# The second kind's attention heads beside the first kind's key and value projections, and the routed rows' queries in plain float32 with ten gather buffers

## The reference, cut to what matters

```python
# 1. first block, attention: two kinds of heads, each 8 heads of 128
q_nope, q_pe = split(rms(cq) @ wq_b)              # first kind: queries, 128 + 64 wide
k_nope, v    = split(rms(ckv) @ wkv_b)            # first kind: keys and values, projected from 512
y_a = softmax(q_a @ k_a.T * A_SCALE) @ v          # first kind
y_b = softmax(q_b @ k_b.T * B_SCALE) @ v_b        # second kind: q_b, k_b, v_b are ready before wkv_b
out = (concat(y_a, y_b) * silu(gate)) @ w_out     # then x = layer_norm(ALPHA * x + g * out)

# 2. last layer of the second block: each row picks 128 expert rows out of 16384
q   = hn @ peer_w_q                               # 2048 -> 8 heads x 128
s1, s2 = q @ sub_keys                             # per head: 2 lists of 128, top 16 of each,
idx = top 16 of the 256 sums                      # 16 experts a head, 128 a row
act = gelu(hn . u_tab[idx]); out = sum(g * act * v_tab[idx])   # 2 x 256 gathers of 128 rows of 8 KB
```

## Time and profile before

| | us |
|---|---|
| median of 3 runs (3640.46 to 3644.57) | 3642.04 |
| profiled execution, its own time | 3634.11 |
| its span | 3632.8 |
| mean granted TensorE clock | 0.864 |

### The profile page before, as it was taken

The page is one execution under the profiler, slowest core; times in us unless marked ns, Lnnn a source line. Parts: engine busy times, 40 slices in busy tenths (PEclk is TensorE's granted clock), DMA queues, the critical chain, the costliest instruction groups (busy, mean ns, idle before and its releaser), DMA issues.

```text
span 3632.8 us, 35860 instructions
## 1 busy us (share of the span) xinstructions
PE 2654.2 (73%) x13396; PEld 2054.7 (57%) x13396; DVE 2679.2 (74%) x3835; ACT 1080.2 (30%) x2010; POOL 1525.5 (42%) x1943
## 2 busy tenths in 40 slices
PE   7989999887999999799978998414434443444445
PEld 6868897455999988598767887401111111111112
DVE  8977887667566655578846555699797888888775
ACT  2255252243444444444664544200000000000000
POOL 7887778740000000000000000277777776767663
PEclk9999999998999999899999999757677766776668
DMA  9876767345376645443124544599999999999998
GB/s 369 319 252 234 247 224 259 144 140 179 107 253 247 219 149 185 174 163 117 70 81 140 185 140 144 199 408 422 422 421 421 416 421 412 423 421 416 422 422 338
DMA packets 277678, 974.09 MB, mean 268 GB/s; under 512 B 14464, under 2 KB 30464, under 8 KB 208384
## 3 DMA queue, kind: packets, MB, share of 16 engines
q0 software_dynamic: 76592, 551.58, 36.8%
q1 hardware_dynamic: 198560, 411.70, 32.4%
q10 hardware_dynamic: 2352, 8.52, 0.7%
HBM read 957.06 MB, written 14.68 MB: 267 GB/s over the span
## 4 chain that ended last, share of the span: by engine, by line
PE 40%; POOL 25%; DMA 17%; DVE 11%; issue 5%; ACT 2%; ACTq 0%; DVEq 0%; POOLq 0%
DMA ring<-in_peer_v,arena 11%; POOL ring L3142 8%; PE lin L486 6%; PE lin L488 6%; PE lin L489 6%; PE lin L2906 5%; PE lin L449 4%; PE lin L450 4%; PE lin L451 4%; DMA ring<-in_peer_u,arena 3%; PE lin L2278 3%; DMA phases<-phase 3%; DVE ring L3063 2%; POOL phase L952 2%; POOL phase L947 2%
## 5 line engine op out<-in xcount | busy, mean ns | idle before, releaser
L2906 PE MATMUL lin<-ring,diag 128*128 128x512 f32 x768 | 535.5, 863 | 732.7 <-DMA ring<-in_peer_v,arena 566.1
L410 DVE TENSOR_TENSOR weight_parts<-ring,weight_parts 128x512 fp32r<-128x512 f32 (+2 forms) x1074 | 709.8, 674 | 489.2 <-ACT weight_parts L398 483.7
L398 ACT CAST weight_parts<-ring 128x512 fp32r<-128x512 f32 (+2 forms) x1074 | 635.7, 599 | 831.1 <-PE lin L489 431.0
L2906 PEld LDWEIGHTS lin<-ring,diag 128*128 128x128 f32 x768 | 207.5, 284 | 1056.0 <-issue 880.0
L3063 DVE CUSTOM_DVE_ANT_0 ring<-ring,arena 128x2048 f32<-128x2048 f32 x256 | 583.4, 2289 | 159.2 <-DMA ring<-in_peer_u,arena 150.9
L486 PE MATMUL lin<-parts,weight_parts 128*128 128x256 f32 x2112 | 611.5, 290 | 47.8 <-DVE weight_parts L410 47.8
L3142 POOL DMA_INDIRECT ring<-in_peer_u,arena x256 | 440.9, 1722 | 402.8 <-DVE arena L2997 254.8
L488 PE MATMUL lin<-parts,weight_parts 128*128 128x256 f32 x2112 | 604.0, 286 | 0.0
L489 PE MATMUL lin<-parts,weight_parts 128*128 128x256 f32 x2112 | 603.8, 286 | 0.0
L3142 POOL DMA_INDIRECT ring<-in_peer_v,arena x256 | 470.9, 1840 | 247.0 <-PE lin L2906 174.6
L2638 POOL DMA_DIRECT2D arena<-mem_keys x1 | 0.6, 575 | 1257.4 <-DVE weight_parts L410 1257.4
(11 more groups left out here) (284 smaller groups left out, 3298.3 us busy)
## 6 DMA issues: line engine op xcount, KB each, us to landing
ring<-in_ada_w SPq DMA_DIRECT2D x96, 1024.0 KB, 8.2
ring<-in_w_in_fourier SPq DMA_DIRECT2D x64, 1024.0 KB, 7.8
ring<-in_w_kv_mem SPq DMA_DIRECT2D x32, 1024.0 KB, 7.7
ring<-in_w_in_attn SPq DMA_DIRECT2D x32, 1024.0 KB, 5.5
ring<-in_w_out_fourier SPq DMA_DIRECT2D x16, 2048.0 KB, 8.0
ring<-in_w_in SPq DMA_DIRECT2D x24, 1024.0 KB, 5.1
ring<-in_w_out_attn SPq DMA_DIRECT2D x8, 2048.0 KB, 8.1
ring<-in_w_out SPq DMA_DIRECT2D x8, 2048.0 KB, 8.1
```

Of the source, the lines that this page charges most:

```text
L398: c.nc.scalar.copy(c.w_parts[:, q, 0, 0:w], c.slot(load, L.kc, w)[:, k % L.kc, :]).then_inc(c.a_high.after(("high", L.name, i)), 1)
L410: c.nc.vector.tensor_tensor(c.w_parts[:, q, 1, 0:w], c.slot(load, L.kc, w)[:, k % L.kc, :], c.w_parts[:, q, 0, 0:w].bitcast(F32), ALU.subt ...
L2906: mm = nc.tensor.matmul(X.sums[t][b][:, :], c.diag[:, X.diag_of(t, k), :], X.bufs[gather_buf(n)][:, b * 512:(b + 1) * 512], start=(k == PE ...
```

## The change

First part. The order of the heads is turned: place n runs head `head(n)`, so places 0 to 7 are the second kind and 8 to 15 the first. Places 0 to 7 stand beside the projections: each has 5 steps of side work, the two key matmul groups or the two value groups of a pair of heads, 5 more steps, and then the place's own head. The rope moves behind place 0, the turns of the queries into places 6 and 7. The later places have 3 + 3 steps for 2 + 2. The scores run one head ahead in places 0 to 7 and two ahead later. SP loads a projection's weights and five (before: four) `ada_w` blocks in turn. The parts of y are split behind places 9, 10 and 13, only part 1 inside `w_out_attn`. x is loaded onto the residual's place, and only the first block's output waits for it.

Second part. The rows are turned first, all 16 blocks; the four query groups use `pe_cols`, each load one unit of the ring. The choice of heads 0 and 1 runs with nothing between, on DVE. The gathers take ten buffers from the first on: four that are free and six ring units as the query groups are done with them. The steps of a choice stand at k = 0, 2, … 18.

```diff
+def head(n):
+    return (n + HEADS) % (2 * HEADS)
 def sp_attention(c):
     for g in range(HEADS // 2):
         yield from sp_load(c, ("wkv_b", g), ...)
-        yield from sp.aside(16)
+        yield from sp.aside(4 * SLOT_STEPS)          # SLOT_STEPS, HEAD_STEPS = 5, 3
...
 def pe_attention(c):
     yield from pe_split_rows(c, X.wq_b, ("cq",), X.cq_rows)
+    yield from pe_scores(c, X, 0)
+    for n in range(HEADS):
+        g = n // 2
+        yield from pe.aside(SLOT_STEPS)
+        yield from (pe_values if n % 2 else pe_keys)(c, X, g)
+        yield from pe.aside(SLOT_STEPS)
+        if n == HEADS - 1:
+            yield from pe_turn(c, "q_pe", ...)
+        yield from pe_turn_probs(c, X, n)
+        if n == HEADS - 2:
+            yield from pe_turn(c, "q_nope", ..., [("attn", "q_roped")])
+        if n == HEADS - 1:
+            yield from pe.wait_ge(*turn_free("q_nope", 8, NT), *turn_free("q_pe", 8, NT), ...)
+        yield from pe_scores(c, X, n + 1)
+        yield from pe_mix(c, X, n)
+    yield from pe_scores(c, X, HEADS + 1)
...
 def v_attention(c):
+    yield from v_scores(c, X, 0)
+    yield from v_normalise(c, X, 0)
+    for n in range(HEADS):
+        yield from v.aside(SLOT_STEPS)
+        yield from v_copy_out(c, key, ...)           # of the keys or the values
+        yield from v.aside(SLOT_STEPS)
+        yield from v_turned_probs(c, X, n)
+        yield from v_scores(c, X, n + 1)
+        yield from v_mixed(c, X, n)
+        yield from v_normalise(c, X, n + 1)
+        if n == 0:
+            ...                                      # rope of the queries
+    low = v_residual_parts(c, c.attn_out.R)
+    for n in range(HEADS, 2 * HEADS):
+        yield from v_turned_probs(c, X, n)
+        ...
+        yield from v.aside(HEAD_STEPS)
+        yield from v_mixed(c, X, n)
+        yield from v.aside(HEAD_STEPS)
+        if n in PART_AFTER:                          # {9: 2, 10: 3, 13: 0}
+            yield from low(PART_AFTER[n])
...
 def g_attention_out(c):
-    yield from c.g.wait_ge(("free", ("mix", 2 * HEADS - 1)))
-    c.nc.gpsimd.dma_start(x, ...)
+    yield from c.g.wait_ge(("full", ("scores", HEADS - 1, NT - 1)))
+    c.nc.gpsimd.dma_start(c.attn_out.H, ...)
 def v_attention_out(c):
-    yield from c.v.wait_ge(("x", "again"))
-    yield from v_split(c, X.L, v_residual_parts(c, X.R), v_gated_residual(...))
+    def out(b):
+        yield from c.v.wait_ge(("x", "again"))
+        yield from residual(b)
+    yield from v_jobs(c, [Job(X.L, out, at={0: lambda b: nothing() if b else low(1)})])
...
 def choice_at(t, k):
-    i = k % (HH * TOPK) - EARLY                      # EARLY = 8
+    i = k % (HH * TOPK)
 def pe_experts(c):
+    for q in range(KD // 4):
+        yield from turn(q)
     for group, L in enumerate(X.q_lins):
-        yield from pe_split_cols(c, L, "ffn_x", X.cols, turn if group == 0 else None)
+        yield from pe_cols(c, L, X.cols, X.parts_turned)
         if group == 0:
             yield from pe_choose(c, X, 0, 0)
 def v_experts(c):
+    for q in range(KD // 4):
+        yield from v_turn_out(c, ("ffn_x", q), ...)
+    yield from v_cols_block(c, X.q_lins[0], ...)(0)
+    v.side = [v_choose(c, X, 0, 0)]
     yield from v.aside(0)
 def g_experts(c):
+    yield from g.wait_ge(("used", last_load(c.memory.L)), ("used", ("parts", c.memory.L.name)),
+                         ("in", last_load(X.q_lins[-1])))
+    for L in X.q_lins:
+        for ch in L.chunks:
+            holder.pop(c.unit_of[(L.name, L.n0, ch)], None)
+            holder[c.unit_of[(L.name, L.n0, ch)]] = ("used", (L.name, L.n0, ch))
+    order = [q for q in range(len(X.bufs)) if q not in holder] + list(holder)
     for n, (t, table, k) in enumerate(ORDER):
-        q = gather_buf(n)
-        yield from g.wait_ge(("used", ("parts", X.q_lins[-1].name)) if n == EARLY else None)
+        q = order[n % len(order)]
+        yield from g.wait_ge(("idx", t, k // (HH * TOPK)), holder.get(q))
```

More of the change, by code:

```diff
@@ L350, in pe_cols @@
             load = (L.name, n, ch)
-            yield from pe.wait_ge(("in", load))
+            yield from pe.wait_ge(("in", load), *ready(ch))
             wt = c.slot(load, L.kc, w)
@@ L1337, in pe_attention @@
     yield from pe_split_rows(c, X.wq_b, ("cq",), X.cq_rows)
[L1338 to L1344, removed]
-            for k in range(4):
[L1346 to L1358, removed]
@@ new lines, in pe_keys, with pe_values @@
+def pe_keys(c, X, g):
+    yield from c.pe.wait_ge(("in", ("wkv_b", g)))
+    wh = kv_weights(c, g)
+    for h in range(2):
+        key = ("ka", 2 * g + h)
+        bank = yield from pe_bank(c, c.lin, key)
+        for k in range(4):
+            mm = c.nc.tensor.matmul(bank[:, :], wh[:, k, h, 0:HD], X.ckvT[:, k, :], start=(k == 0), stop=(k == 3))
+        mm.then_inc(c.pe_full.after(("full", key)), 1)
+def pe_values(c, X, g):
+    wh = kv_weights(c, g)
+    for t in range(0, 4, 2):
+        key = ("va", g, t)
+        bank = yield from pe_bank(c, c.lin, key)
+        for i in range(2):
+            o = bank[:, i * 256:(i + 1) * 256].rearrange("p (h d) -> p h d", h=2)
+            for k in range(4):
+                mm = c.nc.tensor.matmul(o, X.ckvT[:, k, (t + i) * P:(t + i + 1) * P], wh[:, k, :, HD:2 * HD],
+                                        start=(k == 0 and i == 0), stop=(k == 3), skip_group_check=True)
+        mm.then_inc(c.pe_full.after(("full", key), *([("used", ("wkv_b", g))] if t == 2 else [])), 1)
@@ L1820, in a_attention_out, with last_part @@
     X = c.attn_out
[L1821 to L1822 removed]
+    high = a_residual_parts(c, X.R)
+    def last_part(b):
+        if b == 0:
+            yield from c.a.wait_ge(*[("free", ("mix", h)) for h in range(4, 8)])
+            yield from high(1)
+    yield from a_jobs(c, [Job(X.L, nothing, at={0: last_part})])
     yield from a_rstd(c, ("post", 0), st_tmp(c, NT))
@@ L3000, in v_choose, with a_choose @@
     yield from v.wait_ge(step)
-def a_choose(c, X, t, group, steps=0):
+def a_choose(c, X, t, group):
     ks = slice(group * HH * TOPK, (group + 1) * HH * TOPK)
-    for _ in range(steps):
-        yield True
     yield from c.a.wait_ge(("logits", t, group))
```

292 lines of the change are left out of this document (150 added, 142 removed).

## The result

The changed kernel takes 3596.8 us (median of 4 runs, 3593.5 to 3600.0) for 3641.3 (4 runs, 3640.5 to 3644.6): ratio 0.9878, 95% interval 0.9863 to 0.9892, so 44.5 us less. Its profiled execution took 3593.5 (span 3592.1), 40.6 less than that of before. The forecast was 3596, range 3578 to 3621.

What follows compares the result with a forecast made beforehand. It took PE to bound slices 1 to 25 and DMA slices 26 to 40. Attention -17 and experts -29 make -46 on the profiled 3634.1, 3588; plus 7.9 for the median, 3596 us, range 3578 to 3621 with two rivals in.

Steps and rivals of the forecast that it cites:

- Attention: First part, up to the attention output: 799 for 816.65, -17 us, bounds -3 and -25.
- A place: Attention, beside the projections: one place takes 13.3 us, set by DVE, bounds 11.3 and 15; eight take 106.
- moved work: Attention: rope 4.5 us on DVE, two turns 1.5 each, longer first-kind scores at place 7; 12 in all, ending at 708.5.
- POOL's store: End of attention: POOL's phases done at 786 to 794, middle 788; x issued only then, landing at 799, bounds 791 and 807.
- SP's queue: Attention's weight loads: each waits for the ring unit of the one before; taken as nothing, costs 0 to 2 us three times.
- Experts: Second part: gather 32 at 2375.0 for 2406.48, less 2.5 us of queue: -29 us, bounds -41 and +9.
- From there the scores are faster than the queue: Experts from gather 32: a score takes 2.21 us, a gather 2.487, so 480 gathers follow at the queue's pace.
- its own sign of error: Experts: the prediction is wrong if the gathers' queue starves behind gather 45.
- Ten buffers for eight gain nothing in a full queue: Experts' gathers: the two extra buffers were counted as worth nothing.
- (b): Rival: the gathers' queue is not starved and x is early, -41 - 20, 3581 us; 14%.
- (c): Rival: queries at 1.2 GHz, groups 1 to 3 take 81.8 us, gather 32 at 2416, sum -8, 3634; 8%.
- (d): Rival: attention's places at 1.2 GHz, 22.6 us each on PE, output at 870, sum +25, 3667 us; 4%.

Runs made afterwards that it cites:

- e5: The changed kernel run again, unaltered: 3603.6 us for 3635.3, ratio 0.9908.
- e1: The kernel before with only the attention half of the change: 3622.0 us for 3639.1, ratio 0.9952.
- e10: e4 run again, unaltered, on the chip of e9: 3586.1 us, ratio 0.9852.
- e3: The changed kernel with the second choice's key scores computed on PE behind query group 2 instead of 3: 3590.8 us, ratio 0.9865.
- e6: The changed kernel with eight buffers for the gathers instead of ten: 3606.0 us, ratio 0.9915.
- e7: The changed kernel with 4 + 4 side steps in the projections' places and beside later heads, for 5 + 5 and 3 + 3: 3597.8 us, ratio 0.9892.
- e4: The changed kernel with the second choice's key scores computed on PE behind query group 1 instead of 3: 3589.0 us, ratio 0.9864.
- e9: e4 with DVE doing the second choice's first five steps between the first choice and gather 0's landing: 3584.4 us, ratio 0.9854.
- e2: The kernel before with only the experts half of the change: 3610.0 us, ratio 0.9923.
- e12: The changed kernel with only x's load moved from POOL to ACT, behind the exp of the last head: 3594.5 us, ratio 0.9873.
- e11: e9 with x's load issued by ACT behind the exp of the last head instead of by POOL: 3580.3 us, ratio 0.9838.

## Why the prediction was right

*The sum.* The forecast was made for the profiled execution, 3634.1 - 46 = 3588, and 7.9 us were put on it because the median of before lay that much above its profile. The profiled execution took 3593.5, so the change gave 40.6 for 46 (3.9 of the 5.4 too little are the experts'); but its median lies only 3.3 above it. Two errors of 5 us cancel, and that the median is within 1 us of 3596 is luck. The other comparison (e5) has 3603.6, still in the range.

*Attention, -17 forecast, -17.1 measured (e1).* That the two agree to 0.1 is luck too: at the norm the first profile is 15.9 us earlier than before, e1's 12.4 and e5's 6.8. The working holds as a sum, less so in its terms. A place was put at 13.3 us, DVE-set; the first seven took 14.8 on the mean, 10.7 us too long together. Of that 4.5 are the rope, which the prediction booked under moved work, and about 6 are 1.2 GHz in the second and fourth place (0.18 below full over 18.6 and 15.2 us), by estimate; in e5, with less of it, the mean is 14.1. DVE didn't set every place: the fifth and the sixth took 12.1 and 12.3 us with PE busy 12.1 and 11.7 of it and DVE 10.3 and 11.2. Places and moved work ended at 709.6 for 708.5. The last gate came at 773.8 for 771.5, x landed at 797.7 for 799. POOL's store was put at 788 and came at 783.6; x was issued at 784.2 and took 13.4 us, longer than the 9 to 12 allowed. Over the nine executions of this attention with POOL's load the issue lies between 783.2 and 799.5, and in e10 x landed at 809.6, behind the bound of 807. The wait that the prediction made the end of the stage was 0.7 us, since block 0 was ready just then; x was not late at all in e3, e5, e6 and e7, by 1.3 to 2.3 us in e1, e4 and e9, by 11.7 in e10. POOL's small products, 0.366 and 0.245 us in the windows of the earlier trace rows, take 0.298 and 0.299 in the same windows; split where the places end, at 709, they take 0.319 beside the places and 0.270 behind them. SP's queue cost 0 to 1 us three times (0.96 and 0.28 us for `wkv_b`), as bounded.

*Experts, -29 forecast, -29.1 measured (e2), -25.1 between the two first profiles.* Gather 0 came at 2267.32 for 2267, DVE stood 16.54 for 16, gather 32 came at 2358.84 for 2358: the chain was right link by link (a query group took 13.9 to 14.0 us for 13.6, and the first had no slow start). Against the norm gather 32 was 31.7 us earlier than before (31.5 forecast). One term was mis-sized, what is lost again behind it: 6.6 us for 2.5. "From there the scores are faster than the queue" was wrong for 70 us more. DVE was still behind and had the third choice, 17 us, to do: behind gather 45 the queue lacked another 4.6 us (1.8 to 4.5 behind the first 100 us over six executions of this code), which the prediction named as its own sign of error. e2 has 28.0 in its trace for 25.1, 1.7 of it from the second turn: 1.94 us there and 3.57 here, at 1.2 GHz (42.9 for 41.2 in the table). "Ten buffers for eight gain nothing in a full queue" was wrong by 2 to 6 us (e6), since the queue isn't full until 2430; they are part of the right sum, for gather 32 was worked out with ten.

*Rivals.* (b), the queue never starved, was not this kernel, but e4 shows what it is worth: 13.9 us in the trace for the 12 priced. (c) didn't come: the queries ran at 1.00. (d) came in part: the second and fourth place had 0.82, and the stretch 710 to 770 loses, by windows of 10 us, 0 to 7 us to 1.2 GHz from one execution with five steps to the next, and 11 with four. The prediction took 1.00 from one trace and gave this no spread. The rule of the Trainium skill (TensorE: Matmul & The Clock Gate, "A second HAM failure mode: psum-queue depth-cycling"), which it set aside on the strength of that 1.00, says that short idles between groups of matmuls can make the clock go up and down. The trace of e5 agrees with it better than the earlier trace rows did: its windows of 10 us from 710 on have 0.70, 0.96, 0.83, 1.00 and 0.83. The first profile and e12, whose PE program is the same there, have 1.00 from 710 to 760, so the rule doesn't tell when. The other rule of the Trainium skill (SBUF — State Buffer, "SBUF: two separate sides"), a lock for the whole instruction, gave x at 791 to 796 and a sum 3 us better; POOL's store at 783.6 agrees with it, x's landing at 797.7 doesn't, for its load took longer, nor does the store at 798.9 in e10. No run here separates the lock from the density.

## What to carry to other kernels

When work is taken off the front of a chain, look at what the freed engine does next: here 16.5 us of DVE's stand came from an order in PE's program, and the few lines that move it were worth another 12 to 14 us in the profiles and 14 between e12 and e11. A queue that is full in the end can still lack transfers now and then over 160 us at its start; sum what it lacks from windows of equal length: over the six executions of this experts' code it is 16.8 to 19.1 us, where the medians of one kernel move by 7. A sum and its base have to be checked apart, or two errors that cancel look like a good forecast. A load whose issue stands behind an engine's long side work should be issued by whoever first knows that its place is free; here that took away a wait of 0 to 11.7 us in the profiles, though no median shows it.

## What the runs showed of the hardware

- One program's stages move between executions: the first key matmul 584.7 to 590.5, keys to last gate 186 to 195 with the new attention, first output to norm 1423.8 and 1428.0 with the old one (before, e2) and 1423 to 1432 with the new. Norm to gather 0 had two values only with the new experts (42.9, and 41.2 or 41.3), and norm to last row repeated within 3 us over the six executions of the same experts' code (1347.5 to 1350.4), within 1 us between e4 and e10.
- The granted clock of the same stretch (710 to 730) was 1.00, 0.83 and 0.69 in the changed kernel, e5 and e7, with PE busy 14.8, 14.4 and 15.4 of 20 us.
- With DVE at 9.9 of 10 us the gathers still ran at 422 GB/s (e4).
